# Two score levels of a gated linear attention head as one matmul level, and the head's outputs one slot later

## The reference, cut to what matters

```
b     = cumsum(g_)                                   # log decay inside a chunk
decay = exp(where(causal, b[i] - b[j], -inf))
A     = einsum('bhid,bhjd,bhijd->bhij', q_, k_, decay)
out   = einsum('bhij,bhje->bhie', A, v_) + einsum('bhid,bhde->bhie', q_ * exp(b), S)
S_new = exp(b_last) * S + einsum('bhjd,bhje->bhde', k_ * exp(b_last - b), v_)
```

## Time and profile before

| what | value |
|---|---|
| three runs | 891.71, 892.19, 892.40; median 892.19 |
| the profiled execution's own time | 891.21 |
| its span, first to last instruction | 889.4 |
| mean granted TensorE clock | 0.997 of full speed |
| TensorE matmul busy | 878.2 (99% of the span) |
| VectorE busy | 601.5 (68%) |
| ScalarE busy | 412.7 (46%) |
| hosting groups, from about 290 to 687 | TensorE busy at 10 tenths in nearly every slice |

### The profile page before, as it was taken

How to read it: one execution, slowest core, us unless ns; L and a number is a source line. 1 busy time by engine, 2 the same in 40 slices (tenths; PEclk the granted TensorE clock), 3 DMA queues, 4 the chain that set the end, 5 groups by cost and what they waited for, 6 DMA issues and landing times.

```text
span 889.4 us, 11634 instructions
## 1 busy us (share of the span) xinstructions
PE 878.2 (99%) x4323; PEld 730.9 (82%) x4323; DVE 601.5 (68%) x982; ACT 412.7 (46%) x554; POOL 84.9 (10%) x125
## 2 busy tenths in 40 slices
PE   8999999999999999999999999999999999999996
PEld 5887888888888888888888888888888888888885
DVE  6732477733586837487887877888884768556757
ACT  6521532324444334173454654744654455335544
POOL 3010111110000001011111100000111110000000
PEclk9999999999999999999999999999999999999998
DMA  7386679988655756577765654544776888855554
GB/s 269 97 272 200 187 195 220 202 201 247 219 186 164 228 151 198 161 177 149 161 158 137 132 178 142 157 139 165 158 150 145 245 223 270 301 202 188 199 179 189
DMA packets 75164, 167.64 MB, mean 188 GB/s; under 512 B 7333, under 2 KB 15561, under 8 KB 73961
## 3 DMA queue, kind: packets, MB, share of 16 engines
q1 hardware_dynamic: 45266, 108.02, 36.0%
q0 software_dynamic: 16896, 50.34, 26.4%
q10 hardware_dynamic: 12952, 8.61, 3.4%
HBM read 158.56 MB, written 58.72 MB: 244 GB/s over the span
## 4 chain that ended last, share of the span: by engine, by line
PE 92%; DVE 4%; ACT 2%; DMA 1%; issue 1%; ACTq 0%; DVEq 0%
PE main L551 57%; PE main L798 8%; PE main L739 5%; PE sc L798 4%; PE sc L605 4%; PE st L798 2%; PE po L798 2%; PE sc L597 2%; PE po L632 2%; PE sc L739 1%; PE po L635 1%; PE st L617 1%; DMA raw<-in_w_in 1%; PE main L662 1%; PE st L739 1%
## 5 line engine op out<-in xcount | busy, mean ns | idle before, releaser
L551 PE MATMUL main<-h_hi,w_hi 128*128 128x512 f32 x640 | 261.0, 408 | 0.1
L551 PE MATMUL main<-h_hi,w_lo 128*128 128x512 f32 x640 | 250.3, 391 | 0.0
L551 PE MATMUL main<-h_lo,w_hi 128*128 128x512 f32 x640 | 249.8, 390 | 0.0
L1230 DVE TENSOR_TENSOR w_lo<-raw,w_hi 128x1024 fp32r<-128x1024 f32 x102 | 124.6, 1222 | 118.9 <-ACT w_hi L840 118.0
L840 ACT ACTIVATE w_hi<-raw 128x1024 fp32r<-128x1024 f32 x102 | 107.7, 1057 | 205.8 <-PE main L551 161.8
L551 PEld LDWEIGHTS main<-h_hi,w_lo 128*128 128x128 f32 x640 | 120.1, 188 | 26.8
L551 PEld LDWEIGHTS main<-h_lo,w_hi 128*128 128x128 f32 x640 | 120.6, 188 | 21.9
L551 PEld LDWEIGHTS main<-h_hi,w_hi 128*128 128x128 f32 x640 | 120.5, 188 | 21.8 <-issue 0.5
L861 ACT ACTIVATE ex<-ex 128x512 f32<-128x512 f32 (+2 forms) x84 | 52.0, 640 | 60.3 <-DVE ex L1360 48.0
L1691 DVE TENSOR_TENSOR w_lo<-feat,w_hi 128x1024 fp32r<-128x1024 f32 x26 | 31.8, 1224 | 28.1 <-ACT w_hi L1154 27.9
L551 PE MATMUL main<-w_hi,h_hi 128*128 128x512 f32 x128 | 50.6, 396 | 0.0
(11 more groups left out here) (302 smaller groups left out, 1525.3 us busy)
## 6 DMA issues: line engine op xcount, KB each, us to landing
raw<-in_w_in SPq DMA_DIRECT2D x104, 512.0 KB, 4.6
w_sum<-in_w_out POOLq DMA_DIRECT2D x48, 512.0 KB, 5.0
w_sum<-in_w_in POOLq DMA_DIRECT2D x24, 512.0 KB, 5.8
w_sum<-w_sum POOLq DMA_DIRECT2D x24, 512.0 KB, 5.7
raw<-w_sum SPq DMA_DIRECT2D x24, 512.0 KB, 4.0
feat<-w_sum SPq DMA_DIRECT2D x24, 512.0 KB, 4.2
raw<-in_w_out SPq DMA_DIRECT2D x14, 512.0 KB, 4.3
feat<-in_x SPq DMA_DIRECT2D x6, 1024.0 KB, 7.4
```

The lines of the kernel that those rows point to most:

```text
L551: mm = pe.matmul(main[c][:, :], a, b, start=(k == 0 and j == 0), stop=(k == KT - 1 and j == 2))
L1230: dve.tensor_tensor(w_lo[:, q % SPL, :, :], raw[:, q % RAW, :, :], w_hi[:, q % SPL, :, :], ALU.subtract).then_inc(lo_ok, 1)
```

## The change

Levels 4 and 5 become one level. VectorE's two `scale` steps write their keys into the two halves of each chunk of `kl[1]` and their queries into the two halves of each chunk of `ql[0]`. TensorE multiplies 128 keys by 128 queries per chunk, in four matmuls. The three copies to `att` read the two diagonal quarters of the product. `NL` falls from 6 to 5. In the tables the new level stands behind the slot that level 5 had, the outputs stand one slot further on (but for O[1] of the first group, which keeps slot 24), and some M entries move too. On VectorE the second `scale` moves ahead of the copy of level 3, and the next head's `args` ahead of the copies of the merged level. ScalarE's list is the same.

```
-KEYS = [P, P - 4, P - 4, P - 16, P // 2 + 2, P // 2 + 2]
+KEYS = [P, P - 4, P - 4, P - 16, P]
-KL = [0, 1, 1, 0, 1, 0]
+KL = [0, 1, 1, 0, 1]
...
-                        w = P if l == 0 else P // 2
-                        m, at_key = KEYS[l], P // 2 if l == PACKED else P
+                        w = P // 2 if l == 3 else P
+                        m, at_key = KEYS[l], P
...
-            alone = dict(T=7, L=[9, 11, 12, 14, 16, 17], U=[13, 22], O=[19, 24], M=28)
+            alone = dict(T=7, L=[9, 11, 12, 14, 17], U=[13, 22], O=[20, 24], M=28)
...
-            earlier = alone | dict(U=[13, 20], O=[19, 22], M=26)
+            earlier = alone | dict(U=[13, 21], O=[20, 23], M=27)
...
-                    todo |= head_tasks(hg_at(m, u) | dict(T=z, L=[z + 1] + [y + q for q in (3, 4, 6, 8, 9)], U=[z + 3],
-                                                          O=[y + 10], M=y + 14))
+                    todo |= head_tasks(hg_at(m, u) | dict(T=z, L=[z + 1] + [y + q for q in (3, 4, 6, 9)], U=[z + 3],
+                                                          O=[y + 11], M=y + 14 + u))
...
+                    def half(ap):
+                        v = ap.rearrange("p (c h n) -> p c h n", h=2, n=P // 2)[:, :, l - PACKED, :]
+                        return v.rearrange("p c (b s) -> p c b s", s=s)
...
+                    dve.tensor_tensor(half(kl[1][:, :]), chunks(kh), chunks(ek), ALU.mult)
+                    mm = dve.tensor_tensor(half(queries(PACKED)[:, :]), chunks(qh), chunks(eq), ALU.mult)
+                    if l > PACKED:
+                        mm.then_inc(lvl_ok, 1)
...
+                        s = LV[PACKED]
+                        for b in range(2):
+                            to = att[2 * b * s:(2 * b + 1) * s, :].rearrange("p (c n) -> p c n", c=NT)
+                            got = sc[l % 2][b * s:(b + 1) * s, :].rearrange("p (c n) -> p c n", c=NT)
+                            dve.tensor_copy(to[:, :, (2 * b + 1) * s:(2 * b + 2) * s], got[:, :, b * s:(b + 1) * s])
                         s = P // 2
                         _, a = halves(att[0:s, :], s)
-                        got = sc[l % 2][0:s, 0:T // 2].rearrange("p (b s) -> p b s", s=s)
+                        _, got = halves(sc[l % 2][s:P, :], s)
                         dve.tensor_copy(a, got).then_inc(sc_ok, 1)
...
-                        2: [cp(1), cp(2), sl(4), g["states"](0), cp(3), sl(5)],
-                        3: [cp(4), cp(5)], 5: [g["states"](1), g["cut"]], 7: [g["norm"]]}
+                        2: [cp(1), cp(2), sl(4), g["states"](0), sl(5), cp(3)],
+                        3: [cp(4)], 5: [g["states"](1), g["cut"]], 7: [g["norm"]]}
```

More of the change, by code:

```diff
@@ L56 @@
 LV = {3: 16, 4: 32, 5: 64}
-NL, PACKED = 6, 4
+NL, PACKED = 5, 4
 NEXP, NARG = 9, 7
@@ L761, in both @@
                 return {z: a.get(z, []) + b.get(z, []) for z in a | b}
-            alone = dict(T=7, L=[9, 11, 12, 14, 16, 17], U=[13, 22], O=[19, 24], M=28)
-            shared = dict(T=0, L=[1, 4, 5, 7, 9, 10], U=[3, 12], O=[11, 15], M=20)
-            second = dict(T=17, L=[18, 20, 21, 23, 25, 26], U=[20], O=[27], M=31)
-            earlier = alone | dict(U=[13, 20], O=[19, 22], M=26)
+            alone = dict(T=7, L=[9, 11, 12, 14, 17], U=[13, 22], O=[20, 24], M=28)
+            shared = dict(T=0, L=[1, 4, 5, 7, 10], U=[3, 13], O=[12, 16], M=21)
+            second = dict(T=17, L=[18, 20, 21, 23, 26], U=[20], O=[28], M=31)
+            earlier = alone | dict(U=[13, 21], O=[20, 23], M=27)
             group(G_C, False, head_tasks(gla_at(0) | alone))
@@ L1329, in scores @@
                                                 got).then_inc(quad_ok if v < 2 else sc_ok, 1)
[L1330 to L1338, removed]
+                    elif l == 3:
                         s, m = LV[l], KEYS[l]
                         _, a = halves(att[0:m, :], s)
-                        got = sc[l % 2][0:m, 0:T // 2].rearrange("p (b s) -> p b s", s=s)
+                        got = sc[1][0:m, 0:T // 2].rearrange("p (b s) -> p b s", s=s)
                         dve.copy_predicated(a, mask16[0:m, :].rearrange("p (b s) -> p b s", s=s),
@@ L1609, in shared_steps @@
                 return {0: [g["quads"], ar(4), cp(0), sl(3), ar(5)],
-                        1: [cp(1), cp(2), sl(4), g["states"](0), cp(3), sl(5)],
-                        2: [cp(4), s["args"], cp(5), s["ends"]], 3: [g["states"](1), s["early"], g["cut"]],
+                        1: [cp(1), cp(2), sl(4), g["states"](0), sl(5), cp(3)],
+                        2: [s["args"], cp(4), s["ends"]], 3: [g["states"](1), s["early"], g["cut"]],
                         4: [s["quads"], ar2(4), cp2(0), sl2(3), ar2(5)],
-                        5: [cp2(1), cp2(2), sl2(4), s["states"](0), cp2(3), sl2(5), g["norm"]],
-                        6: [cp2(4), nxt["args"], cp2(5), nxt["ends"], nxt["early"], s["cut"]], "end": [s["norm"]]}
+                        5: [cp2(1), cp2(2), sl2(4), s["states"](0), sl2(5), cp2(3), g["norm"]],
+                        6: [nxt["args"], cp2(4), nxt["ends"], nxt["early"], s["cut"]], "end": [s["norm"]]}
             group(G_C, gla_steps(0), lambda c: None)
@@ L1628, in hg_pair @@
                     todo[z] = [h["quads"], ar(4), cp(0), sl(3), ar(5)]
-                    todo[z + 1] = [cp(1), cp(2), sl(4), h["states"](0), cp(3), sl(5)]
-                    todo[z + 2] = ([cp(4)] + [x["args"] for x in nxt] + [cp(5)]
+                    todo[z + 1] = [cp(1), cp(2), sl(4), h["states"](0), sl(5), cp(3)]
+                    todo[z + 2] = ([x["args"] for x in nxt] + [cp(4)]
                                    + [f for x in nxt for f in (x["ends"], x["early"])] + [h["cut"]])
```

14 lines of the change are left out of this document (8 added, 6 removed).

## The result

| kernel | median us | runs | lowest to highest |
|---|---|---|---|
| before | 892.12 | 20 | 890.90 to 897.27 |
| after | 893.35 | 20 | 892.50 to 896.86 |

The ratio is 1.0015, 95% interval [1.0008, 1.0021]: slower by 1.2 us. That is inside the 0.2% that was called no change, but the sign is the other one, the forecast of 891.8 is 1.5 too low, and the time lies just outside the range (893.2).

A forecast was written before the change was run, and what follows sets the result against it. TensorE's own work, busy 99% of the span, was taken to bound the kernel. 891.21 - 2.16 + 1.37 + 0.41 = 890.83, with 0.98 to the median 891.8 us; 8-in-10 range 890.2 to 893.2, own range 891.2 to 892.6.

The forecast's parts named there:

- The two blocks that go: 2.16: TensorE's score blocks: two at 0.54 replaced by one at 0.90, gaining 0.18 per head, 2.16 us for 12 heads.
- VectorE's part: VectorE's four scale steps and three copies keep their durations; the next head's scan runs while VectorE would wait for the level.
- rival of longer copies: VectorE's copies of the merged level take longer, up to 1.0 us in all, giving up to 897.0; chance 0.10.
- The second group's end: 1.37: End of second hosting group: O[1] 1.19 later delays ScalarE's stores and TensorE's next group, costing 1.37 us.
- The fourth group's end: 0.41: End of fourth group: late outputs delay the stores; TensorE waits 0.33 plus 0.08 of restart, costing 0.41 us.
- The mean square of a pair's first head: First head of each pair: VectorE's copies start later, yet the mean square is ready 0.07 early, three times; cost 0.
- The ends of the pairs' groups: Pairs' group ends: VectorE's chain to the gate within 0.05 of before, next matmul in time by 0.2; cost 0.
- Level 1 in the shared groups: Second head's level 1 in shared groups: ScalarE's later take of O[1] still leaves 0.07, twice; cost 0.
- I take 0 for them: The last three kinds of place (pairs' group ends, mean squares, level 1) hold barely and add 0 to the sum.

The follow-up runs named there:

- the shift alone: Kernel before, levels 4 and 5 still apart, with only the change's tables of updates, outputs and mean squares: 894.06 us, ratio 1.0012.
- putting it back: Changed kernel with the second hosting group's update, outputs and mean square back in their old slots: 892.35 us, ratio 0.9997 to the kernel before.
- the shorter chain: Changed kernel with the next head's level 3 exponent subtractions moved behind the cut on VectorE: 892.21 us, ratio 1.0007 to the kernel before.
- the run with 66 keys: Merged level one slot earlier, all else in old slots, but the merged level multiplies only 66 of 128 keys: 891.68 us, one run.

## Why the prediction was wrong

Point by point, by its own steps:

- *The two blocks that go: 2.16.* Right in kind and 0.44 too small: 2.60 in the trace where nothing else moves. Both blocks of 66 by 64 were taken at 0.54 and the new one at 0.90. From level 4 to the outputs before has 3.84 for two slots and both blocks (586.33 to 590.17), which is 0.54 and 0.56; the merged level takes 3.63 for two slots and one block of 0.89. That is 0.21 a head. The reason given was not complete. The phrase that "a good part of a block does not follow its columns" is too much: a block follows its larger side, and the two blocks save little more than one fixed part, by an estimate about 0.17 (the line through 0.54 at 66 and 0.89 at 128).
- *VectorE's part.* Same durations, as taken: 0.58 for the two copies and 0.43 for the third, in before 0.58 and 0.42. The rival of longer copies did not happen, by starts either (0.59 and 0.35, before 0.61 and 0.34).
- *The second group's end: 1.37.* Right: +1.36 with the shift alone, 1.33 by putting it back.
- *The fourth group's end: 0.41.* Right with the shift alone, +0.41. In the changed kernel the group gives +0.07 where +0.05 was forecast, but by another way: the distance before the first pair's group is only 0.32 (511.82 to 512.14), 0.09 of wait and 0.08 of restart, under the 0.2 to 0.5 that was to show there. The late mean square just before it, which was not foreseen, takes 0.23. ScalarE's chain ends when it was said to end, so a delay ahead of it only takes the place of a part of this wait.
- *The mean square of a pair's first head: "It holds by 0.07, three times".* This is the step that failed. Two terms of 0.1 were missing. The copies were called "0.85 long", but by the starts of VectorE's instructions in before they take 0.61 for the two and 0.34 for the third, 0.95 (587.11 to 587.72 and 589.03 to 589.37, in the same timeline as the earlier trace rows). The cut begins 0.45 after the subtraction before it (598.08, 598.53), in before 0.34. With 0.09 and 0.11 a slack of 0.07 becomes a delay of 0.13, and 0.16 is measured; 0.11 of restart comes on top. The same place in the second heads of the two shared groups (450.98, 511.48) wasn't looked at, and it is late too.
- *The ends of the pairs' groups: "It holds by 0.2".* Failed for the same reason. "VectorE's chain to the gate comes out within 0.05" was wrong: the scan has moved into the wait, but the copies wait for the level after it. Lined up by TensorE's mean square (569.91, in before 566.67 and one slot less 0.18 later, a shift of 2.05), the step after the copies starts 0.27 later than in before (561.37 against 559.05) and the cut adds 0.11, so the gate comes 0.39 later. From gate to matmul it is 0.82 and not the 0.75 taken. TensorE, whose regular start would be 570.37, starts at 570.53. This is 0.16 and 0.17 late at two places, 0.08 of restart at each.
- *Level 1 in the shared groups: "It holds by 0.07, twice".* Also gone, by little: TensorE's distances there are 0.30 (at 429.95) and 0.26 (at 490.47), so 0.07 and 0.03 late. These two hang on the outputs' slot too: with the merged level early or the chain shorter they are still 0.04 to 0.10 late, and with the level early and all old slots they are not.
- *"I take 0 for them."* The forecast's own range had 0.15 at each of five such places at its high end, 892.6. In truth there were nine (five mean squares, two gates, two levels), and the mean squares and gates also pay the restart. An answer that hangs on TensorE's own earlier work moves with TensorE: what was gained or lost before a head does not make its places less late, and each group loses anew. The first two pairs' groups show it: +0.07 each, for a forecast of -0.36, and -0.44 each where the level is early. By the distances the nine places cost 1.79; the fourth group's wait is 0.24 under the forecast and the blocks give 0.44 more. This makes 1.11 of the error of 1.19.

So the sum erred in two terms of opposite sign, the blocks' gain, too small by 0.44, and the tight places, taken at 0. The size of the error says less than the places do: with the merged level one slot earlier the trace gives -0.59 against -0.38, and the nearness of the two is in part luck, since the blocks' 0.44 more is half eaten again. What made the kernel slower than forecast is the delay in VectorE's chain, and the shorter chain takes 1.08 of it back. Of the 1.5 between forecast and median the trace has 1.19; the rest, some 0.3, lies between the median of 20 runs and one trace, and I can't assign it.

What stays open is why the cut starts 0.45 after the subtraction in every kernel with the merged level but the shorter chain, the ones without a gap too, and 0.34 in before and with the slots alone, where the outputs are as late. Its wait on the squares isn't the reason by the trace of the changed kernel: ScalarE had written them by 596.98, 1.5 ahead of the cut. In the shorter chain the cut follows another instruction, and there is no such excess. No kernel was made for this alone.

## What to carry to other kernels

Where TensorE is 99% busy, list every place where it takes an answer from another engine whose chain the change lengthens, in each kind of group, and measure the slack by starts, not by durations: VectorE's records here overlap by up to 0.09 or leave up to 0.17 between them, and a slack of 0.07 over a chain of 17 instructions is none. Count such places at their full number, each with a restart of 0.1, and charge them in every group, since the answer moves with TensorE: here nine such places ate most of the gain of twelve heads. A freed slot on TensorE is best given to the step that the longest chain hangs on: the same merge with the level one slot earlier and the outputs where they were is 0.3% quicker than before, the change as made 0.15% slower.

## What the hardware showed

- A block of eight float32 matmul records costs by the larger of its two sides: 0.54 to 0.56 for 66 by 64, 0.82 for 112 by 64, 0.89 to 0.92 for 128 by 128, 66 by 128 and 128 by 64.
- A TensorE that has waited ahead of a matmul with 512 moving columns, even for 0.05 (570.02 in the shorter chain), starts its second one 0.30 to 0.34 after the first and not 0.23: each such wait costs 0.07 to 0.11 more than itself.
- From the start of a 0.69 subtraction on VectorE to TensorE's use of its result it is 0.74 (598.53 to 599.27); from the start of a 0.5 store on ScalarE to the matmul that it releases, also 0.74 (390.25 to 390.99); from the start of a gate on VectorE, 0.82 (569.71 to 570.53).
- Eleven traces, with nearly the same code ahead of the heads, reached the first transposes between 292.54 (before) and 295.53 (the run with 66 keys), and TensorE waits up to 1.1 there for VectorE's keys. One trace says no more than this of when the heads begin.
